# Twenty projection products moved within each head of a delta rule, one ScalarE copy put behind four others, and the requests' states stored one by one

## The reference, cut to what matters

```python
h = rms(x)*g0*(1+scale1)+shift1
qkv_pre, z, b, a, q_nsa, kv_nsa, g_nsa, g_merge = _split(h @ w_in, IN_SIZES)
q, k, v = split(silu(conv(qkv_pre)))          # q, k normalised; 8 heads, 128 wide
# per head, prompt cut into chunks (here 4 of 128 tokens):
lower = strict_lower(kb @ k.T * decay)        # kb = k * beta
u, w  = solve(I + lower, [v*beta, kb*exp(g)])
v_new = u - w @ S
o     = (q*exp(g)) @ S + (q @ k.T * decay) @ v_new
S     = S*exp(g_last) + (k*exp(g_last-g)).T @ v_new
o     = o * rsqrt(mean(o*o) + eps) * onorm_g * silu(z)
```

## Time and profile before

| | us |
|---|---|
| median of 3 runs | 1923.19 |
| lowest, highest | 1921.03, 2191.4 |
| profiled execution | 1924.08 |
| its span | 1922.6 |
| deltanet, eight heads | 133.0 to 701.3 of the span |
| request_delta | 701.3 to 857 of the span |

### The profile page before, as it was taken

The page is one execution under the profiler, slowest core; times in us unless marked ns, Lnnn a source line. Parts: engine busy times, 40 slices in busy tenths (PEclk is TensorE's granted clock), DMA queues, the critical chain, the costliest instruction groups (busy, mean ns, idle before and its releaser), DMA issues. The chain is left out here.

```text
span 1922.6 us, 30114 instructions
## 1 busy us (share of the span) xinstructions
PE 1680.5 (87%) x11733; PEld 1484.7 (77%) x11733; DVE 744.9 (39%) x1290; ACT 549.8 (29%) x890; POOL 162.6 (8%) x177
## 2 busy tenths in 40 slices
PE   4899889889889889977788899898985899997996
PEld 2598888888888879866574454458985899997996
DVE  1244554554553421323414434434435333332223
ACT  3243333333333320210003333323133434332222
POOL 0012322322312201100000000000000000000000
PEclk9799989989999986986879999999997899998997
DMA  6422212212112132437532343244212233332211
GB/s 188 114 71 73 70 33 79 63 33 85 57 33 98 45 86 80 140 121 226 155 110 88 110 153 121 94 136 167 98 44 89 66 89 99 96 87 90 90 60 45
DMA packets 228688, 181.72 MB, mean 95 GB/s; under 512 B 8566, under 2 KB 221039, under 8 KB 228425
## 3 DMA queue, kind: packets, MB, share of 16 engines
q1 hardware_dynamic: 203434, 161.82, 27.8%
q10 hardware_dynamic: 25184, 18.96, 3.2%
HBM read 166.31 MB, written 23.02 MB: 98 GB/s over the span
## 5 line engine op out<-in xcount | busy, mean ns | idle before, releaser
L704 PE MATMUL dn_pg<-proj_xh,dn_wh 128*128 128x260 f32 x832 | 184.0, 297 | 6.5 <-DVE dn_wl L1003 6.0
L704 PE MATMUL dn_pg<-proj_xh,dn_wl 128*128 128x260 f32 x832 | 182.5, 296 | 0.0
L704 PE MATMUL dn_pg<-proj_xl,dn_wh 128*128 128x260 f32 x832 | 179.1, 293 | 0.0
L251 PE MATMUL gu_ps<-fh_xh,gu_wh 128*128 128x260 f32 x704 | 142.4, 284 | 19.1 <-DVE gu_wl L310 19.1
L251 PE MATMUL gu_ps<-fh_xh,gu_wl 128*128 128x260 f32 x704 | 142.4, 284 | 0.0
L251 PE MATMUL gu_ps<-fh_xl,gu_wh 128*128 128x260 f32 x704 | 142.3, 284 | 0.0
L704 PEld LDWEIGHTS dn_pg<-proj_xh,dn_wh 128*128 128x128 f32 x832 | 134.3, 195 | 8.3 <-DVE dn_wl L1003 7.1
L704 PEld LDWEIGHTS dn_pg<-proj_xh,dn_wl 128*128 128x128 f32 x832 | 134.2, 195 | 0.0
L704 PEld LDWEIGHTS dn_pg<-proj_xl,dn_wh 128*128 128x128 f32 x832 | 134.2, 195 | 0.0
L251 PEld LDWEIGHTS gu_ps<-fh_xh,gu_wh 128*128 128x128 f32 x704 | 109.2, 190 | 19.5 <-issue 19.5
L251 PEld LDWEIGHTS gu_ps<-fh_xh,gu_wl 128*128 128x128 f32 x704 | 109.2, 190 | 0.0
(11 more groups left out here) (472 smaller groups left out, 3381.3 us busy)
## 6 DMA issues: line engine op xcount, KB each, us to landing
all_ring<-in_w_gu SPq DMA_DIRECT2D x44, 512.0 KB, 5.0
all_ring<-in_w_in SPq DMA_DIRECT2D x32, 512.0 KB, 6.9
att_ada<-in_w_ada SPq DMA_DIRECT2D x16, 1024.0 KB, 5.3
fd_ring<-in_w_down SPq DMA_DIRECT2D x8, 1408.0 KB, 6.2
all_ring<-in_w_in SPq DMA_DIRECT2D x10, 1024.0 KB, 5.3
fr_ada<-in_w_ada SPq DMA_DIRECT2D x8, 1024.0 KB, 8.7
dn_xs<-in_w_in SPq DMA_DIRECT2D x16, 512.0 KB, 3.7
all_ring<-in_cmp_w ACTq DMA_DIRECT2D x16, 512.0 KB, 4.5
```

What stands on the lines that cost most here:

```text
L251: last = pe.matmul(self.ps[:, j, c, 0:HALF], w[:, j, k, :], x[:, k0 + k, c * HALF:(c + 1) * HALF], start=(k0 + k == 0 and w is self.wh and ...
L704: last = pe.matmul(pg[:, j, c, 0:HALF], w[:, j, k, :], x[:, k, c * HALF:(c + 1) * HALF], start=(k == 0 and term == 0), stop=(k == KD - 1 a ...
```

## The change

Three edits.

1. The table `BITES`: "scaled" 80 instead of 100, "kk" 22 instead of 12. The sum is 10 less in front, and these ten stand at the end of the head, in the rest ahead of L794.
2. On ScalarE `take(h1, 1)` (for the last head `keep_last(1)`) stands behind the four copies of the turned operands.
3. `store` sends the states of one request (512 KB) instead of four (2 MB). Stores 0 to 3 stand behind the loads 4 to 7, the other four at the end.

```diff
-BITES = {"scaled": 100, "turned": 6, "kk": 12, "hop": 7}
+BITES = {"scaled": 80, "turned": 6, "kk": 22, "hop": 7}
...
                 if more:
                     take(h1, 0)
                     split_high(h1, 2)
-                    take(h1, 1)
                 else:
                     keep_last(0)
                     split_last(2)
-                    keep_last(1)
                 for n, (bank, dst) in enumerate(((Dp, knT), (B, kbT), (A, qnT), (C, qgT))):
                     a.wait_ge(turned, 4 * h + n + 1 + START)
                     a.activation(dst[:], bank[:], ACT.Copy).then_inc(ch_ready, 1)
                 if more:
+                    take(h1, 1)
                     split_high(h1, 3)
                 else:
+                    keep_last(1)
                     split_last(3)
...
-            def store(n):
+            def store(b):
                 for s in range(2):
-                    sp.wait_ge(updated[s], 16 * (n + 1) + START)
-                sp.dma_start(io["s_delta"][0, n * 4:(n + 1) * 4].rearrange("b h k v -> k (b h) v"),
-                             S[:, n * 32:(n + 1) * 32]).then_inc(stored, 16)
+                    sp.wait_ge(updated[s], 4 * (b + 1) + START)
+                sp.dma_start(io["s_delta"][0, b].rearrange("h k v -> k h v"), S[:, b * H:(b + 1) * H]).then_inc(stored, 16)
 
             for t in range(2, TILES // 2):
                 load(t)
-            store(0)
-            store(1)
-            sp.wait_ge(stored, 32 + START)
+                if t >= 4:
+                    store(t - 4)
+            for b in range(TILES // 2 - 4, NB):
+                store(b)
+            sp.wait_ge(stored, 16 * NB + START)
```

## The result

Four runs of the changed kernel took 1892.17 to 1903.09 us, **1899.24 us** at the median; the kernel before took 1923.74 beside them (one of its four executions, at 2191.4 us, does not count in the ratio). The ratio is 0.9875, with a 95% interval of 0.9841 to 0.9909: about 24 us less, within 2%. The profiled execution took 1901.74 us (span 1900.3). The forecast of 1899 us is met. The sum behind it is met less well: the delta rule gave 12.5 us of the 22.1 forecast, and some 6 us came from stages that the change does not touch.

The account below looks back on a forecast made before the run. TensorE is nearly always busy, so only its idle gaps, low clock and a stage-end transfer wait give time. 15.5 + 4.1 + 2.5 + 3.2 = 25.3 us off 1924.1 gives 1899 us; range 1890 to 1911.

Parts of the forecast that it names:

- the 22.1 forecast: Delta rule's share of the predicted gain: 15.5 us from moved products, 4.1 and 2.5 us from the clock.
- Ahead of L736: Turned keys: 20 fewer products ahead start L736 2.40 us earlier in two heads, 1.79 in six; 15.5 us in all.
- the heads of the second kind: The six heads represented by head 1, where L736 was to start 1.79 us earlier, not 2.40.
- Ahead of L748 and the ScalarE copy: First inverse factor: the 1.60 us wait hides ten products, keeping 0.4 us; tile 1's later copy costs nothing.
- The clock at the head's end: L796 to next head: a 1.55 us wait keeps the full clock in six heads, 0.68 us each, 4.1 us.
- The last head: Low clock behind L748 goes, 2.5 us taken between 0 and 3.4; ten later products land among its levels.
- Level 4: The 1.67 us wait at L763 stays; clock falls behind it counted as 0 us, bounds -6 to +5.
- the 68 to 70.5: Sign that the prediction holds: seven heads of the delta rule take 68 to 70.5 us.
- The stores: End of requests' stage: the last gate lands earlier behind a 0.5 MB store, 3.2 us gained, bounds 0 and 3.4.
- the clock gives nothing back: Rival, delta rule: no gain from the clock, 1905.4 us, or 1910 with three more level 4 falls; chance 0.19.
- the wait only moves: Rival, ahead of L736: scaled operands come later and L736 starts where it did, 1921 us; chance 0.06.
- ScalarE comes late: Rival, first X: copy queued behind take and split, TensorE stands at L763 in every head, slower; chance 0.03.

Follow-up runs that it names:

- e10: The kernel before with ten idle matmuls put in the 2.76 us wait ahead of L796 of heads 0 to 6; 1912.78 us, ratio 0.9954.
- e3: The changed kernel with 12 products instead of 22 behind L742, and ScalarE's first extra tile copy behind that of nwT; 1900.07 us, ratio 0.9893.
- e5: The kernel before with only ScalarE's copy of tile 1 moved behind the four turned copies; 1923.19 us, ratio 0.9989.
- e1: The kernel before with only the new stores of the states, one a request; 1918.71 us, ratio 0.9989.
- e9: The kernel of e6 with 32 products instead of 22 behind L742, taken from the head's end; 1882.35 us, ratio 0.9795.
- e6: The changed kernel with three ScalarE steps (a split; silu and copy of tile 2) moved behind X copies of levels 3 and 4; 1865.99 us, ratio 0.9719.
- e11: The changed kernel with ten idle matmuls put in the 1.67 us wait for level 4's X of heads 0 to 6; 1886.72 us, ratio 0.9823.
- e2: The changed kernel with the old stores: only the moved products and the ScalarE copy; 1899.65 us, ratio 0.9893.
- e8: The changed kernel with 60 products instead of 80 ahead of L736, and ScalarE's first extra tile copy behind that of nwT; 1951.05 us, ratio 1.0147.

## Why the prediction was right, step by step

**Ahead of L736: right in mechanism, 1.2 us too high.** The move is 15.06 - 13.27 = 1.79 us a head between kernels whose heads begin at the full clock (e10 and the change). That is the figure the prediction had for the heads of the second kind. The 2.40 us for heads 2 and 4 held 0.6 us of another thing: these heads ran longer at 1.2 GHz at their start and so brought TensorE later to L736. With 1.6 us in the last head, all eight give 14.2 us where 15.5 stood.

**Ahead of L748 and the ScalarE copy: right.** e3 gives the ten products back and loses nothing; e5 moves the copy and changes nothing. The waits came out at 0.4 us before L748, 0.63 before L736 and 1.57 before L796, against 0.4, 0.6 and 1.55.

**The clock at the head's end: right, and worth more.** e10 shows it without a product moved. A head of before that falls at level 4 loses 72.16 - 71.15 = 1.0 us by it, one that does not 71.19 - 69.55 = 1.6. The prediction's 0.68 a head counted only from L796 to the next head's start and missed what the low clock cost behind it. 4.1 us were forecast, 6.7 measured over the heads 1 to 6.

**The last head: its low stretch right in size, the cause less simple, and a second one missed.** I laid the stretch to the wait of 1.6 us before L748. That wait alone is not enough: in e10 it stands at 1.61 us and the clock is 1.00 behind it, and the head is 3.2 us shorter; in e3 it stands at 1.59 and the head takes 59.4 us, as in the change. In e1 and e5, where the end of head 6 is that of before, the head takes 65.5. So the stretch went with the long idle stretch at the end of head 6. That it hangs on this alone is not shown: head 1 of e5 had both waits before it, at the full clock, and did not fall at L748. In e9 the wait at the end of head 6 is 2.76 us and L748 doesn't wait, and the clock behind L748 is 1.00, but there it had already fallen, behind L796 of head 6:

```profile
626.80:633.60 6.80, 6.76 (x59) 6.59 (x58) 2.24 (x3) 1.29 (x3) 2.04 (x3) 1.00 0.48 145
```

The prediction had no term for the recurrence of the last head. Before, the products ran out ahead of level 5, and the granted clock of the seven us from L773 on was 0.53. In the change seven of the ten later products stand in level 5, L763 doesn't wait there any more, and the clock of the same seven us is 1.00:

```profile
685.40:692.40 7.00, 5.93 (x24) 5.09 (x25) 1.00 (x4) 1.09 (x2) 0.00 (x0) 0.53 0.00 0
```

```profile
673.41:680.41 7.00, 5.61 (x36) 4.54 (x36) 1.72 (x6) 1.09 (x2) 0.00 (x0) 1.00 0.00 0
```

From L773 to the last L790 it is 10.3 us before and in e10, and 8.4 in the change, e3, e6 and e11. So the change took 65.57 - 59.22 = 6.35 us off this head: 1.6 by L736, 3.2 behind L748 and 1.9 in the recurrence, less 0.3 that the later products cost among the levels. Forecast were 1.8 and 2.5, the last with these products in it.

**Level 4: the step that failed.** I took 0 for the falls behind the wait of 1.67 us, with bounds from -6 to +5. Before, four heads paid 1.6 us each, 6.4 in all. After, three paid 1.6 and two 7.4, 19.6 in all. So this profiled execution lost 13.2 us there, more than twice the bound, and the delta rule gave 12.5 us instead of 22.1. The parts measured above come to 14.2 + 6.7 + 3.2 + 1.9 - 0.3 - 13.2 = 12.5, without the end of head 0. Five of the seven heads came out at 67.8 to 69.9 us, near the 68 to 70.5 that the prediction named as a sign; the two at 75 miss it. The bound assumed that a fall costs 1.6 us because the profile of before held no other. e11 shows the cause (the idle time) and e6 the cure. What decides between no fall, a short one and a long one stays open: the wait was 1.67 us in each case, e2 had one long fall in seven heads, the change and e3 two, e10 one in its head 0.

**The stores: right.** 3.2 us forecast, 3.5 measured at TensorE and 3.6 in the stage (155.3 to 151.6). The rule of the Trainium skill (DMA: Bandwidth & Descriptors, "Rules for kernel authors") that asks for larger transfers did not decide here. The eight stores take longer together (8 x 5.6 = 45 us of landings against 2 x 10.9), but nothing waited for them; what counted was the length of the one ahead of the gate.

**The point estimate: partly by errors that cancelled.** Of the 22.3 us between the two profiled executions, 12.5 lie in the delta rule, 3.6 in the requests' stage and 6.2 in stages that the change leaves alone (the attention 4.3, the front 1.4, the others 0.5 together). These 6.2 us were in no term of mine. The median, not this execution, is what hit 1899. The kernel before gave 1912 to 1933 us beside the experiments; that the forecast could start from a profiled execution 0.9 us above the median of three was luck, and the range of 21 us was about as wide as one kernel's own spread.

The rival "the clock gives nothing back" is out by e10, "the wait only moves" by L736 at 13.27 us, "ScalarE comes late" by L763, which waits at no level where it did not before.

## What to carry to other kernels

Where TensorE arrives late at work that another engine has ready, count the cheap filler ahead of it and cut it until the two meet; past that point (e8) each piece removed only makes an idle stretch. Price an idle stretch of TensorE by what the clock does behind it as well as by its length, and give that price the longest fall that could follow, not the one the profile happens to hold. Where such a stretch can't be removed, work that is thrown away can shorten it, but look first for what stands ahead of the releaser in its engine's queue: here three ScalarE operations, each moved behind the copy that TensorE waited for, were worth about as much again as the whole change (a ratio of 0.9719 against its 0.9875).

## What the runs showed of the hardware

- An idle stretch of 1.67 us between full-rate matmuls was followed by no fall, by a low clock that cost 1.6 us, or by one of 17 us that cost 7.4, in the same kernel at the same place. With 0.49 us of idle time there (e11) no head of seven fell.
- The length of the stretch does not settle it: behind 2.76 us the first four matmuls took 1.12 us in six heads before the change and 0.65 to 0.66 in five of seven heads of e9, where the low clock came some matmuls later in three and not at all in two.
- A wait does not by itself explain the low clock behind it: the low stretch behind L748 of the last head is there in the kernel before, e1 and e5, and gone in e10, which only adds matmuls at the ends of the heads before it, with the wait next to it unchanged (1.6 us). How the earlier idle stretch, some 23 us ahead, bears on it is open.
- In the last head the granted clock was 0.53 for the 7 us from L773 on where the products had run out a level earlier and L763 waited for 0.47 us (before, e10), and 1.00 where products ran on into level 5 and it didn't wait (the change), with the later waits of 0.4 to 0.7 us the same in both.
- A transfer of 260 KB from ScalarE's queue landed 2.0 us behind its issue with a store of 0.5 MB issued 4.0 us ahead of it, and 5.5 us behind it with one of 2 MB 3.9 us ahead.
